# The fronts of two mixtures of experts, put in another order: weight halves loaded and split inside the last output unit, rows gathered as soon as ranks are counted, weights of choice worked out beside the gather

## What is computed

```python
def moe_swiglu(xn, router, w_gu, w_down):              # mixture 1, xn = rmsnorm(h, od_norm_moe)
    logits = (xn @ router).astype(jnp.float32)
    top_v, top_i = lax.top_k(logits, TOP_K)            # 2 of 8
    w = jax.nn.softmax(top_v, axis=-1)
    comb = jnp.sum(jax.nn.one_hot(top_i, N_EXPERTS) * w[..., None], axis=-2)
    for e in range(N_EXPERTS):
        out = out + comb[..., e:e + 1] * swiglu(xn, w_gu[e], w_down[e])

def _grouped_moe(x, router_w, router_b, w1, w3, w2):   # mixture 2, x = layer_norm(...)
    scores = sigmoid(xt @ router_w); biased = scores + router_b
    group_sel = argmax(sum of the 2 best of each group of 4)
    2 best experts inside that group; gates = their scores / their sum
    for e in range(N_EXPERTS_2):
        hid = jax.nn.silu(xt @ w1[e]) * (xt @ w3[e])
        out = out + gate_dense[:, e, None] * (hid @ w2[e])
```

## Time and profile before

| | us |
|---|---|
| median of 3 runs (2213.07 to 2215.09) | 2213.98 |
| the profiled execution's own time | 2214.88 |
| its span, first to last instruction | 2213.0 |
| TensorE busy | 2160.9 (98%) |
| VectorE busy | 1726.4 (78%) |
| ScalarE busy | 1360.6 (61%) |
| mixture 1, first expert half to the picks that follow its turns (L2370) | 649.8 to 1601.9 |
| mixture 2, the same | 1923.1 to 2195.3 |

### The profile page before, as it was taken

How to read it: one execution, slowest core, us unless ns; L and a number is a source line. 1 busy time by engine, 2 the same in 40 slices (tenths; PEclk the granted TensorE clock), 3 DMA queues, 4 the chain that set the end, 5 groups by cost and what they waited for, 6 DMA issues and landing times. The chain is left out here.

```text
span 2213.0 us, 30469 instructions
## 1 busy us (share of the span) xinstructions
PE 2160.9 (98%) x11693; PEld 1853.8 (84%) x11693; DVE 1726.4 (78%) x1614; ACT 1360.6 (61%) x1205; POOL 82.4 (4%) x79
## 2 busy tenths in 40 slices
PE   7999999999999999999999999999999999999997
PEld 7988999877878888888888888888889888788886
DVE  4755655798668888888888988888866665698997
ACT  4454433526457777777777777777756344477775
POOL 3000000000000000000000000000000000000000
PEclk9999999999999999999999999999999999999999
DMA  9552555622279999999999999999945161799995
GB/s 304 177 175 95 172 197 183 224 105 85 91 266 377 375 382 380 379 382 375 388 364 392 358 395 365 394 369 385 378 140 175 58 228 39 268 371 382 378 378 226
DMA packets 274824, 617.26 MB, mean 279 GB/s; under 512 B 9536, under 2 KB 34320, under 8 KB 274736
## 3 DMA queue, kind: packets, MB, share of 16 engines
q1 hardware_dynamic: 265648, 584.43, 72.1%
q0 software_dynamic: 9088, 31.60, 4.6%
HBM read 603.41 MB, written 12.58 MB: 278 GB/s over the span
## 5 line engine op out<-in xcount | busy, mean ns | idle before, releaser
L2479 DVE TENSOR_TENSOR w_low<-ring,w_high 128x2048 fp32r<-128x2048 f32 x426 | 971.3, 2290 | 134.6 <-ACT w_high L1734 134.1
L1734 ACT ACTIVATE w_high<-ring 128x2048 fp32r<-128x2048 f32 x426 | 815.1, 1917 | 169.2 <-PE ps L813 169.2
L812 PE MATMUL ps<-w_high,parts 128*128 128x512 f32 (+2 forms) x1896 | 735.8, 388 | 0.0
L811 PE MATMUL ps<-w_high,parts 128*128 128x512 f32 x1560 | 617.7, 396 | 5.4 <-DVE gates L2383 3.9
L813 PE MATMUL ps<-w_low,parts 128*128 128x512 f32 x1560 | 609.0, 390 | 0.0
L812 PEld LDWEIGHTS ps<-w_high,parts 128*128 128x128 f32 x1896 | 356.8, 188 | 69.2
L811 PEld LDWEIGHTS ps<-w_high,parts 128*128 128x128 f32 x1560 | 293.4, 188 | 67.6 <-DVE gates L2383 4.3
L813 PEld LDWEIGHTS ps<-w_low,parts 128*128 128x128 f32 x1560 | 293.2, 188 | 62.8
L1927 DVE TENSOR_TENSOR w_low<-ring,w_high 128x2048 fp32r<-128x2048 f32 (+2 forms) x117 | 262.2, 2253 | 103.8 <-ACT w_high L1450 96.6
L1450 ACT ACTIVATE w_high<-ring 128x2048 fp32r<-128x2048 f32 (+2 forms) x117 | 219.7, 1883 | 134.4 <-PE ps L813 124.5
L811 PE MATMUL ps<-XT_high,w_high 128*128 128x256 f32 x1024 | 293.0, 286 | 7.0 <-DVE parts L1918 5.2
(11 more groups left out here) (441 smaller groups left out, 1620.3 us busy)
## 6 DMA issues: line engine op xcount, KB each, us to landing
ring<-in_od_moe_gu SPq DMA_DIRECT2D x224, 1024.0 KB, 8.2
ring<-in_od_moe_down SPq DMA_DIRECT2D x112, 1024.0 KB, 7.9
ring<-in_w SPq DMA_DIRECT2D x96, 1024.0 KB, 9.1
ring<-in_ev_ffn_gu SPq DMA_DIRECT2D x22, 1024.0 KB, 7.5
ring<-in_xa_wkv SPq DMA_DIRECT2D x8, 2048.0 KB, 8.3
ring<-in_od_pw_w SPq DMA_DIRECT2D x6, 2048.0 KB, 8.3
ring<-in_w_in SPq DMA_DIRECT2D x6, 2048.0 KB, 8.0
ring<-in_ev_ffn_down SPq DMA_DIRECT2D x11, 1024.0 KB, 5.2
```

Of the source, the lines that this page charges most:

```text
L811: mm(out_, xh, wh, start=start, stop=False)
L812: mm(out_, xl, wh, start=False, stop=False)
L1734: A(w_high[:, j % SPLITS, :], ring[:, j % NS, :], ACT.Copy).then_inc(moe_sem(k, "high"), 1)
L2479: V.tensor_tensor(w_low[:, j % SPLITS, :], ring[:, j % NS, :], w_high[:, j % SPLITS, :].bitcast(F32), SUB)\
```

## The change

The tables that don't depend on the logits (`choice_tables`) are made in the attention ahead of mixture 1. SyncE's first group of loads is written out, and each of its first six halves waits only for the dense panel that holds its place in `ring`; the dense panels sit one place further on so that places fall due in order. The first two halves are split inside the last output unit and the third beside the choice. ScalarE loads the tables of the square root and the sigmoid earlier. `ranks` is cut in two: `first_picks` goes right behind the rank matmuls, followed by the gather and the split of its rows, and the weights of choice, the rest of `ranks` and `pick(0)` come after. The row numbers of turn 0 are found behind half 1 (`find_rows(0)`), and turned into places ahead of half 4 (`first_places`). The scaled rows XS are made ahead of halves 9 and 11 of turn 0. The loads of `count` on TensorE, ScalarE and VectorE move behind turn 0. The fillers shrink. GpSimd's program is unchanged.

```diff
+FILL_CHOICE = {1: 18, 2: 22}
+FILL_RANKS = 8
+ROWS_SCALED_AT = 9
...
@@ SyncE
+                        if isinstance(g, int) and j % 2 == 0 and j // 2 < SLOTS:
+                            sync.wait_ge(S(held[j // 2][1]), held[j // 2][2])
                         sync.wait_ge(moe_sem(k, "split"), turn * len(halves) + (j + 1))
...
-                with sync.Fori(0, c["groups"]) as g:
+                group(0, 0)
+                with sync.Fori(1, c["groups"]) as g:
...
-            for i in range(moe1_panel - SLOTS, moe1_panel):
-                sync.wait_ge(S(panels[i][1]), panels[i][2])
@@ TensorE
-                keep_busy(30 if k == 1 else 36, 6)
+                keep_busy(FILL_CHOICE[k], 6)
...
-                    keep_busy(30 if k == 1 else 44, 6)
-                    pe.wait_ge(moe_sem(k, "picked"), turn + 1)
-                    for tc in range(2):
-                        mm(ps[:, 7, 0:FILLED + 1], PR[:, tc, :], CBS[:, tc, :], start=(tc == 0), stop=(tc == 1))
+                    keep_busy(FILL_RANKS, 6)
+                    pe.wait_ge(moe_sem(k, "picked"), 1)
...
+                        if first and j < 2:
+                            pe.wait_ge(moe_sem(k, "gathered_split"), j + 1)
...
+                        if first and j == 1:
+                            find_rows(0)
@@ ScalarE
-                act.wait_ge(moe_sem(k, "read"), j + 1)
+                act.wait_ge(S("parts_read"), moe_parts[k] - SPLITS + (j + 1))
...
+            first_high(1, 0)
+            first_high(1, 1)
             columns_high(("od_norm_moe", 0), 0)
+            A(table_root, ONES[:, 0:1], ACT.Sqrt)
...
+            first_high(1, 2)
             act.wait_ge(S("exp_wanted"), 1)
             A(PAIRW[:, 1, :], PAIRW[:, 0, :], ACT.Exp).then_inc(S("exp_ready"), 1)
-            for j in range(SPLITS):
-                first_high(1, j)
...
             columns_high(None)
+            A(table_root, ONES[:, 0:1], ACT.Sigmoid)
             logit_rows(2)
@@ VectorE
                 lows(halves_to(f"{tag}q1", 4))
+                if tag != "A":
+                    first_low("ABC".index(tag), 0)
                 for j in range(2):
                     add_unit(f"{tag}o{j}", j, ALPHA if tag == "C" else None)
+                    if j == 0 and tag != "A":
+                        first_low("ABC".index(tag), 1)
...
+            first_picks(1)
+            first_low(1, 2)
+            first_gathered_low(1)
             dve.wait_ge(S("exp_ready"), 1)
...
                     for j in range(N):
+                        if first and j == 4:
+                            first_places()
+                        if first and k == 1 and j == ROWS_SCALED_AT:
+                            rows_scaled(0)
+                        if first and k == 1 and j == ROWS_SCALED_AT + 2:
+                            use_row(0, rows_scaled(1))
+                            dve.sem_inc(S("xs_ready"), 1)
                         if j == PICK_AT:
                             pick(it + 1)
                         if j == MOVE_AT:
```

More of the change, by code:

```diff
@@ L470, in load, with experts @@
                     sync.dma_start(dst, src).then_inc(S(f"landed{slot(i)}"), 16)
-            def experts(k, source):
+            def experts(k, source, panels_before):
                 c = MOES[k]
                 slots, halves = c["slots"], stream(c)
+                held = {slot(i): panels[i] for i in range(panels_before - SLOTS, panels_before)}
                 sync.sem_inc(moe_sem(k, "split"), slots)
@@ L1077, in find_rows @@
                 def find_rows(turn):
-                    pe.wait_ge(moe_sem(k, "picked"), turn + 1)
+                    pe.wait_ge(moe_sem(k, "picked"), turn + 2)
                     for tc in range(2):
@@ L1112, in experts @@
                 pe.sem_inc(moe_sem(k, "read"), SPLITS)
-                gather(0)
-                pe.wait_ge(S("turns_ready"), k)
-                turns = pe.value_load(count[0:1, k - 1:k], min_val=c["groups"], max_val=2 * c["groups"])
+                gather()
                 def a_turn(it):
-                    pe.wait_ge(moe_sem(k, "gathered_split"), it + 1)
+                    first = isinstance(it, int)
+                    if not first:
+                        pe.wait_ge(moe_sem(k, "gathered_split"), it + 2)
                     def turn_hidden(ch):
@@ L1832, in _ @@
             A(LG, ps[:, 5, 32:64].rearrange("p (a e) -> p a e", e=16), ACT.Sigmoid).then_inc(S("router_by_act"), 1)
-            for j in range(SPLITS):
-                first_high(2, j)
+            first_high(2, 2)
             experts(2)
@@ L2025, in map_scores, with first_low, choice_tables @@
                 return ps[:, 5:7, :].rearrange("p a (b t) -> p a b t", t=T)
+            def first_low(k, j):
+                dve.wait_ge(moe_sem(k, "high"), j + 1)
+                V.tensor_tensor(w_low[:, j, :], ring[:, j, :], w_high[:, j, :].bitcast(F32), SUB).then_inc(moe_sem(k, "split"), 1)
+            def choice_tables():
+                step(V.tensor_scalar(IOM, c_("iota")[:, 0:16], -99.0, None, ADD))
+                step(V.memset(CBS, 0.0))
+                step(V.tensor_reduce(CBS[:, 0, TOKEN:TOKEN + 1], c_("upto"), X, ADD))
+                for tc in (1, 0):
+                    step(V.tensor_scalar(CBS[:, tc, TOKEN:TOKEN + 1], CBS[:, 0, TOKEN:TOKEN + 1], -1.0, float(P * (tc + 1)), MUL, ADD))
+                step(V.tensor_scalar(CBS[:, :, FILLED:FILLED + 1], CBS[:, :, TOKEN:TOKEN + 1], -UNFILLED, None, ADD))
+                step(V.tensor_scalar(SPARE, CBS[:, 0, TOKEN:TOKEN + 1], float(T), None, ADD))
+                V.tensor_copy(add_at[:, :], SPARE)
             def attention(tag, a, gain):
@@ L2337, in ranks, with first_gathered_low @@
                 step(V.tensor_scalar(RK[:, :, 0:G], RK[:, :, 0:G], -1.0, None, ADD))
+                for tc in range(2):
+                    if k == 1:
+                        last = V.tensor_scalar(w_(256, 2, P)[:, tc, :], c_("iota"), RK[:, tc, 0:1], rstd[:, tc:tc + 1], ALU.is_equal, MUL)
+                    else:
+                        last = V.tensor_scalar(w_(0, 2, P)[:, tc, :], c_("iota"), RK[:, tc, 0:1], None, ALU.is_equal)
+                last.then_inc(moe_sem(k, "picked"), 1)
+            def first_gathered_low(k):
+                for p in range(4):
+                    dve.wait_ge(S("first_gathered_high"), 4 * (k - 1) + p + 1)
+                    src = ps[:, p, 0:2 * P].rearrange("p (k t) -> p k t", t=P)
+                    for i in range(2):
+                        kc = 2 * p + i
+                        if k == 1:
+                            last = V.scalar_tensor_tensor(x_low[:, kc, :], src[:, i, :], vec("od_norm_moe", kc), x_high[:, kc, :].bitcast(F32), MUL, SUB)
+                        else:
+                            last = V.tensor_tensor(x_low[:, kc, :], src[:, i, :], x_high[:, kc, :].bitcast(F32), SUB)
+                    if p % 2:
+                        last.then_inc(moe_sem(k, "gathered_split"), 1)
+            def ranks(k):
+                c = MOES[k]
+                G, M = c["groups"], c["members"]
                 V.tensor_scalar(RK[:, :, G:2 * G], RK[:, :, 0:G], -float(P), None, ADD)
@@ L2346, in ranks @@
                 V.tensor_scalar(count[:, k - 1:k], CMAX, float(G), None, ADD).then_inc(S("turns_ready"), 1)
-            def first_low(k, j):
-                dve.wait_ge(moe_sem(k, "high"), j + 1)
-                V.tensor_tensor(w_low[:, j, :], ring[:, j, :], w_high[:, j, :].bitcast(F32), SUB).then_inc(moe_sem(k, "split"), 1)
             def experts(k, dst):
@@ L2362, in pick @@
                     for tc in range(2):
-                        V.tensor_copy(CBS[:, tc, 0:M], CB[:, tc, bass.ds(turn * M, M)])
+                        last = V.tensor_copy(CBS[:, tc, 0:M], CB[:, tc, bass.ds(turn * M, M)])
+                        if k == 2 and isinstance(turn, int) and turn == 0:
+                            continue
                         last = V.tensor_scalar(PR[:, tc, :], iota, RK[:, tc, bass.ds(turn, 1)], None, ALU.is_equal)
```

76 lines of the change are left out of this document (30 added, 46 removed).

## The result

The changed kernel takes **2236.64 us**, the median of four runs (2235.8 to 2238.26), against 2213.99 before: a ratio of 1.0101, with a 95% interval of 1.009 to 1.0113. It is slower by 22.7 us, where 5.8 were forecast and the range ended at 2226. Its profiled execution took 2236.61, span 2234.8 (before: 2214.88, span 2213.0).

A forecast was written before the change was run, and what follows sets the result against it. TensorE, busy 98% of the span, sets the turns' pace, so only its idle and slow stretches, mainly the two fronts, could change. Terms: 9.75 + 1.65 − 6.2 + 0.6 = +5.8, median 2219.8 us, range 2213.5 to 2226.

The forecast's parts named there:

- Choice, ranks, picks, split halves: Mixture 1's front: choice starts 0.92 us earlier, picks done at 640.4, gather at 640.45 for 643.77, early splits free.
- half 0 needs only the first four, near 643.7. So half 0 starts at 644.05: Mixture 1's front: half 0 waits only for the first four subtractions of gathered rows; it started at 649.76 before.
- The stall at half 12: Mixture 1, turn 0: late XS, chain of 18.2 us; half 12 at 695.7 for 685.99, 9.7 lost net of front gain.
- Half clock behind the stall: Mixture 1, turn 0: after 16 us of idleness TensorE runs at 1.2 GHz, 1.65 us lost (0 to 3.3).
- Clock in the front of mixture 1: Mixture 1's front: the 2.2 us gap goes, at most 1.1 remains between fillers, so full clock was taken.
- Rival 3: Both fronts: fewer fillers let the clock fall, +1.65 us in mixture 2, less in mixture 1; 2223 us; chance 0.08.
- VectorE's lack of slack from half 8 to 11: Mixture 1, turn 0: the two XS copies add 2 × 1.23 us to VectorE, which ends half 11 at 676.7.
- Stall at find_rows in mixture 2: Mixture 2's front: TensorE stands 0.6 us at find_rows while VectorE finishes weights, counting and the pick at 1922.1.
- Loads of `turns`: End of turn 0, both mixtures: loads moved out of the fronts cost 0.3 us each, 0.6 in all.
- The 6.2 for mixture 2: Mixture 2's front: earlier gather and half 0 bring half 4 to 1928.1 for 1934.23, 6.2 us won.
- Rival 2: Mixture 1, turn 0: scatter has landed when VectorE reaches the place move, no stall; 2202.3 us; chance 0.08.
- rival 1: Mixture 1, turn 0: same stall, but store and scatter meet empty queues, chain 14.4 for 18.2 us; 2216.0 us; chance 0.16.

The follow-up runs named there:

- e5_fill: e3_both with 24 and 30 idle matrices ahead of the ranks instead of 18 and 22: 2205.03 us.
- e10_signals_xs: e1_signals with the two copies of XS back ahead of turn 0, places still moved at half 12: 2204.12 us, ratio 0.995 to the kernel before.
- e1_signals: The change with VectorE's two signals (banks 0 and 1 free) sent ahead of the first picks instead of behind the weights, both mixtures: 2225.3 us.
- e4_before_xs: The kernel before, with only the two copies of XS moved to halves 9 and 11 of turn 0: 2234.3 us, ratio 1.0087.
- e2_late_move: The change with turn 0 of mixture 1 moving places at half 20 and asking for rows at half 23, not 12 and 13: 2218.93 us.
- e6_xs_front: e3_both with the two copies of XS back ahead of turn 0, behind the first pick: 2205.29 us.
- e8_load_front: e3_both with TensorE's wait for the number of turns and its load back between gather and half 0, both mixtures: 2219.43 us.
- e3_both: The change with the edits of e1_signals and e2_late_move together: 2206.06 us, ratio 0.9959 to the kernel before.
- e7_move14: The change with turn 0 of mixture 1 moving places at half 14 and asking for rows at half 15: 2233.12 us.

## Why the prediction was wrong

- **Choice, ranks, picks, split halves:** right. Predicted from the logits' matmuls to half 0 of mixture 1: 644.05 − 634.59 = 9.46. In e5_fill, with the signals moved, more idle matrices and a full clock, it is 642.97 − 633.49 = 9.48. In mixture 2, from its first idle matrices to half 0: predicted 1916.15 − 1893.25 = 22.90; in e10_signals_xs 1911.94 − 1889.07 = 22.87.
- **The step that failed: "half 0 needs only the first four, near 643.7. So half 0 starts at 644.05",** and the same step in mixture 2. I took the gathered rows for the last of half 0's waits. It also waits for `silu`, whose first signal stands in `experts`, which VectorE now reaches only behind the weights and the counts. In the kernel before it stood at the same line, and the weights were long done by then. The diff does not touch that line; it moves what is ahead of it. Measured: 648.12 in mixture 1, 4.1 late, and 1940.82 in mixture 2, where 1935.3 was due (22.9 behind 1912.44), 5.5 late. Of the 4.1, the signals are 3.3: in e10_signals_xs, with the same clock in the gather and the signals moved, half 0 starts at 644.85. e1_signals takes these waits away, and with them 11.3 us of the 16.9 by which the median missed; it ends at 2225.3, inside the forecast's range.
- **The stall at half 12:** right in mechanism and nearly in size. XS was done at 678.36 for 674.4, which is half 0's delay. The chain took 19.2 for 18.2: the store 10.7 to its landing for the 8.5 that I took, the scatter 5.9 for 7.1. Both landings were missed, and the sum came out near because the two errors are of opposite sign, which is luck. Half 12 came at 700.58 for 695.7, and 4 of these 4.9 us are half 0's delay again. e4_before_xs shows the stall by itself, e2_late_move what its absence gives.
- **Half clock behind the stall:** 2.0 for 1.65. **Behind idleness in mixture 2:** nothing was forecast, since no idleness was; two halves took 2.9 more than at full clock.
- **Clock in the front of mixture 1:** I took full clock, and most of the gather ran at half. This cost about 1.6 in the change, although half 0 waited for the signals and not for the rows: VectorE splits the gathered rows before it comes to the weights, so the signals came later too. From the logits' matmuls to the end of the last count it took 14.3 in the change (633.78 to 648.09) and 12.7 in e5_fill (633.49 to 646.16), where the gather was at full clock. Rival 3, the cold fronts, had the fall in mixture 1 right. In mixture 2 the gather ran at full clock (3.84), and the fall came behind the wait for the signals.
- **VectorE's lack of slack from half 8 to 11:** the two copies cost TensorE 0.7 there, and the 2.5 that I charged were VectorE's, for the end of XS. What I did not see is that in the front they cost nothing (e6_xs_front).
- **Stall at find_rows in mixture 2, 0.6:** not there in e10_signals_xs (half 0 at 1911.94, find_rows at 1917.59). **Loads of `turns`, 0.6:** no idle time shows behind turn 0, so 0; in front of half 0, in e8_load_front, 0.85 to 1.0 passed.
- **Not forecast:** turns 1 to 7 take 119.35 each instead of 119.18 (GpSimd's scatters, 791.34 to 1507.46 for 774.78 to 1489.87), 1.0 in all. The extra 0.15 lies once in each turn, between halves 7 and 8, with no wait shown. The same period is in e3_both, 119.30 and 119.27 are in e1_signals and e10_signals_xs, and e4_before_xs has none of it (119.17). Its cause was not tried. Another 1.5 came between 1747 and 1757 of the kernel before, where both kernels run the same code and both fall to the lower clock, in the changed kernel for longer (granted 0.62 and 0.70 over 5 us each, for 0.76 and 0.90). The 0.7 behind the last transposes was not looked into.
- **The miss of 16.0 in the profiled execution, in parts.** The signals: 3.3 in mixture 1, 5.2 and 2.9 of half clock in mixture 2. The rest: the gather's clock 1.6, the chain 1.0, half clock behind the stall 0.3, the turns' period 1.0, the stretch near 1750 1.5, the end 0.7; less 0.8 by which the logits came earlier, and less the 0.6 of the loads. That is 16.1. Only the signals' part was taken away by an edit; the others are read from the traces. (The 6.2 for mixture 2 is 6.13 by its own working, and the 9.75 is 9.7; nothing turns on it.)
- **Rivals.** Rival 2, no stall, did not come about in the change; e10_signals_xs has no stall and ends near its number (2204.12 for 2202.3), but by early copies, which the rival did not have. The short chain of rival 1, 14.4, was seen in no run: 17.9 (e1_signals) to 20.0 (e7_move14) where VectorE waited for it.
- **The Trainium skill against the rows.** The Trainium skill, DMA: Bandwidth & Descriptors, section "Anatomy of one DMA — SWDGE (gpsimd) path", would by my estimate from its figures give the store 4.4 and the scatter 3.2. The stores of XS landed in 10.7 (the change), 9.4 (e4_before_xs) and 7.0 (e10_signals_xs), the scatters in 5.9, 6.2 and 10.1. The measurement decides: these transfers took 1.6 to 3.2 times what that rule gives.

## What to carry to other kernels

When a diff moves work ahead of a line that it does not touch, look at what else stands at that line. Signals that hand over a free buffer cost nothing and look like nothing, and the waits on the other engine should be listed one by one, each with the instruction that ends it and what now stands ahead of it in that queue. Work that feeds a chain of transfers should be moved later only with the end of the chain in view: here 2.5 us of VectorE, which cost nothing where they were, released a chain of 18 to 20 us, and its only consumer did not move. Where such a consumer must wait, ask first whether it is needed so soon: moving it eight halves later took an edit of two lines.

## What the runs showed that I had not expected

- **A signal is in the queue like any instruction.** TensorE's half 0 started 0.03 after VectorE's last count had ended, and 3.5 after the data that it needs was split. VectorE seems to finish its work before it sends these signals: the vector instruction behind them started 0.22 after the start of the last count (647.94, 648.16), where it is 0.07 in e3_both (648.19, 648.26), whose signals stand elsewhere. The Trainium skill, PSUM — Partial Sum Buffer, section "Engine vs sequencer instructions", says that VectorE's queue is strictly first in, first out; this trace agrees. It also says that an increment on an instruction of the sequencer alone can fire while the work ahead of it is still in flight; no run here shows that.
- **The clock in a front falls at another time in each execution.** With nearly the same code ahead of it, TensorE was at 1.2 GHz from about 634 to 644 (e1_signals), 636 to 639 (e6_xs_front), 640 to 643 (the change, e3_both and e10_signals_xs), and not at all (e5_fill). With the lower clock in most of it the gather takes 5.4 to 5.5, at the full one 3.8. The runs of one kernel spread over 2 to 5 us with it: e2_late_move ranged from 2216.1 at a mean clock of 0.994 to 2221.4 at 0.990. The Trainium skill, TensorE: Matmul & The Clock Gate, section "What's actually happening", says of a kernel's start that the number of matmuls at the lower clock varies from run to run for the same kernel. No run here shows the start of one kernel twice; what these traces show is the like of it amid the kernel, between kernels that differ little.
- **A landing took longer with loads beside it.** The scatter of turn 0 took 5.9 to 6.2 where TensorE stood still and the ring had nothing to load (the change, e1_signals, e4_before_xs), 7.8 with two halves more (e7_move14), and 9.7 to 11.2 in the nine kernels, the one before among them, where the loads went on. The store of XS took 6.7 to 7.0 when issued in the front and 9.0 to 10.7 when issued in the loop.
